# A recurrent mixer's key, reception and value projections computed from high and low parts

## The reference, cut to what matters

```python
def rwkv7_time_mix(h, mix, ...):
    xx = jnp.pad(h, ((0, 0), (1, 0), (0, 0)))[:, :-1] - h
    xr, xw, xk, xv, xa, xg = [h + xx * mix[i] for i in range(6)]
    r = (xr @ w_r).astype(f32)          # 256x1024 @ 1024x1024
    k = (xk @ w_k).astype(f32)
    v = (xv @ w_v).astype(f32)
    w_log = -jax.nn.softplus(-(w0 + jnp.tanh(xw @ w1) @ w2).astype(f32)) - 0.5
    a = jax.nn.sigmoid((a0 + (xa @ a1) @ a2).astype(f32))
    ...
    kk = kk / jnp.maximum(jnp.sqrt(jnp.sum(kk * kk, axis=-1, keepdims=True)), 1e-12)
    k = k * (1.0 + (a - 1.0) * k_a.astype(f32))
    _, y = lax.scan(rwkv7_step, ...)
    ...
    y = y + (jnp.sum(r_h * k_h * r_k, axis=-1, keepdims=True) * v_h).reshape(B, S, D)
```

## Time and profile before

| what | value |
|---|---|
| median of 3 runs | 2742.5 us (2739.02 to 2743.58) |
| profiled execution, span from its first to its last instruction | 2735.7 us |
| what the median has beside that span | 6.8 us |
| PE busy over the span | 98% |
| DVE / ACT / POOL busy | 77% / 47% / 4% |
| the stage, from the first key matmul to the last of `products(0, 1)` | 754.7 to 854.7 us |

### The profile page before, as it was taken

The page is one execution under the profiler, slowest core; times in us unless marked ns, Lnnn a source line. Parts: engine busy times, 40 slices in busy tenths (PEclk is TensorE's granted clock), DMA queues, the critical chain, the costliest instruction groups (busy, mean ns, idle before and its releaser), DMA issues.

```text
span 2735.7 us, 51145 instructions
## 1 busy us (share of the span) xinstructions
PE 2687.7 (98%) x20542; PEld 2491.8 (91%) x20542; DVE 2119.8 (77%) x3212; ACT 1291.1 (47%) x1781; POOL 109.8 (4%) x109
## 2 busy tenths in 40 slices
PE   8999999999999999999999999999999999999999
PEld 7998799999988989999869999986899999859999
DVE  7985589889764647984977878599777787987777
ACT  5335553443442325335565544556554464464443
POOL 0000000000013310000000000000000000000000
PEclk9999999999999999999999999999999999999999
DMA  7764267667431015764424455441345544404454
GB/s 269 277 230 154 85 261 273 228 251 277 160 129 74 1 69 222 276 233 166 157 74 154 169 184 184 155 146 55 109 164 181 180 161 146 154 16 150 158 184 154
DMA packets 61230, 456.21 MB, mean 167 GB/s; under 512 B 6840, under 2 KB 6864, under 8 KB 8736
## 3 DMA queue, kind: packets, MB, share of 16 engines
q1 hardware_dynamic: 54432, 395.83, 40.0%
q0 software_dynamic: 6656, 58.35, 5.3%
HBM read 453.09 MB, written 1.07 MB: 166 GB/s over the span
## 4 chain that ended last, share of the span: by engine, by line
PE 88%; DVE 5%; ACT 3%; DMA 2%; issue 1%; DVEq 0%; SPq 0%; ACTq 0%
PE ps L762 21%; PE ps L601 14%; PE ps L602 14%; PE ps L603 14%; PE ps L1043 3%; PE ps L1440 3%; DMA ring<-in_weights 2%; PE ps L1447 1%; ACT arena L2076 1%; PE ps L1299 1%; PE ps L1133 1%; PE ps L1126 1%; PE ps L544 1%; PE ps L1282 1%; PE ps L537 1%
## 5 line engine op out<-in xcount | busy, mean ns | idle before, releaser
L1612 ACT ACTIVATE w_parts<-ring 128x1024 fp32r<-128x1024 f32 x462 | 462.9, 1052 | 408.3 <-PE ps L601 315.5
L2147 DVE SCALAR_TENSOR_TENSOR w_parts<-ring,w_parts 128x1024 fp32r<-128x1024 f32 x462 | 544.6, 1219 | 53.5 <-ACT w_parts L1612 53.2
L762 PE MATMUL ps<-stream_high,half_parts 128*128 128x256 f32 x2224 | 427.0, 288 | 2.1 <-DVE half_parts L2352 2.1
L2352 DVE SCALAR_TENSOR_TENSOR half_parts<-ring,half_parts 128x1024 fp32r<-128x1024 f32 x225 | 271.8, 1212 | 135.9 <-ACT half_parts L1699 135.0
L762 PEld LDWEIGHTS ps<-stream_high,half_parts 128*128 128x128 f32 x2224 | 351.9, 190 | 7.5 <-issue 6.7
L601 PE MATMUL ps<-act_parts,w_parts 128*128 128x256 f32 x1232 | 347.1, 282 | 1.6 <-DVE w_parts L2147 1.3
L601 PE MATMUL ps<-h_parts,w_parts 128*128 128x256 f32 x1200 | 340.8, 284 | 7.8 <-DVE w_parts L2147 7.8
L603 PE MATMUL ps<-act_parts,w_parts 128*128 128x256 f32 x1232 | 348.0, 282 | 0.0
L602 PE MATMUL ps<-act_parts,w_parts 128*128 128x256 f32 x1232 | 347.5, 282 | 0.0
L602 PE MATMUL ps<-h_parts,w_parts 128*128 128x256 f32 x1200 | 339.5, 283 | 0.0
L603 PE MATMUL ps<-h_parts,w_parts 128*128 128x256 f32 x1200 | 339.5, 283 | 0.0
(11 more groups left out here) (462 smaller groups left out, 5185.3 us busy)
## 6 DMA issues: line engine op xcount, KB each, us to landing
ring<-in_weights SPq DMA_DIRECT2D x374, 1024.0 KB, 4.8
arena<-in_mod_weights POOLq DMA_DIRECT2D x32, 1536.0 KB, 8.2
arena<-in_cond POOLq DMA_DIRECT2D x8, 512.0 KB, 6.4
arena<-toeplitz_rows POOLq DMA_DIRECT2D x1, 1536.0 KB, 12.3
x<-in_x SPq DMA_DIRECT2D x1, 1024.0 KB, 4.9
arena<-in_ctx POOLq DMA_DIRECT2D x1, 1024.0 KB, 5.5
out<-x SPq DMA_DIRECT2D x1, 1024.0 KB, 3.9
const<-in_const SPq DMA_DIRECT2D x1, 975.0 KB, 11.3
```

What stands on the lines that cost most here:

```text
L762: mm = pe.matmul(into, stationary, moving, start=start and n == 0, stop=stop and n == 2, skip_group_check=True)
L1612: a(w_parts[:, to, 0, cols], ring[:, at, cols], ACT.Copy).then_inc(s["w_high"], 1)
L2147: return stt(out=out, in0=whole, scalar=1.0, in1=high, op0=ALU.mult, op1=ALU.subtract)
L2352: stt(out=half_parts[:, u % 3, 1, :], in0=ring[:, (t["tile"] + tile) % RING, half * HALF:(half + 1) * HALF], scalar=1.0, in1=half_parts[:, ...
```

## The change

The three projections become sums of three fp32r products, like the others. Per half tile (128 x 1024, eight blocks; 24 of them):

- ACT copies the half tile into one of three buffers `rw_high` (`weight_highs`), once the tile has landed and, from the fourth on, once PE has begun the half tile before the last (`half_used`).
- DVE subtracts it and writes the rest over the weights in the ring (`weight_lows`, `ring_low` is the ring's own memory seen as fp32r).
- PE runs 24 products in place of eight matmuls, after waiting for `half_low`.

The moving side (the mixed tokens) is split by DVE, four copies and four subtractions per projection (`split_mixed`). The calls are laid into the queues by hand, and `keep(4, 3)` and `mix(4, 3)` move behind the key's evacuation. The small table of ones moves to memory of `h` (`key_spread`).

```diff
+        ring_low = nc.alloc_sbuf_tensor_at("ring_low", [P, RING, TILE], F32R, offset=ring_at)
+        rw_high = [parts("rw_high0", 29760, HALF), parts("rw_high1", 20992, HALF), parts("rw_high2", 22016, HALF)]
+        mixed_parts = {2: (parts("key_high", 2048, KT, S), parts("key_low", 0, KT, S)),
+                       3: (parts("reception_high", 25120, KT, S), parts("reception_low", 18944, KT, S)),
+                       4: (parts("value_high", 0, KT, S), nc.alloc_sbuf_tensor_at("value_low", [P, KT, S], F32R, offset=half_at))}
...
-                def project(i, p):
+                def project_parts(i, p):
+                    high, low = mixed_parts[i]
                     for m in range(2):
+                        u = 8 * (i - 2) + 2 * p + m
+                        pe.wait_ge(s["half_low"], RW_FIRST + u + 1)
                         for k in range(KT):
+                            if p == m == 0 and k % 2 == 0:
+                                pe.wait_ge(s["mix_ready"], LOW_AT[i] + k // 2 + 1)
...
-                            mm = pe.matmul(ps[:, mm_n[0] % 4, m * S:(m + 1) * S], w.take(), mixed[i][:, k, :], start=(k == 0), stop=(k == KT - 1))
+                            w.used(pe.matmul(into, wh, high[:, k, :], start=(k == 0), stop=False, skip_group_check=True))
+                            mm = pe.matmul(into, wh, low[:, k, :], start=False, stop=False, skip_group_check=True)
+                            if k == 0:
+                                mm.then_inc(s["half_used"], 1)
+                            mm = pe.matmul(into, wl, high[:, k, :], start=False, stop=(k == KT - 1), skip_group_check=True)
...
+                def weight_highs(upto):
+                    while split[0] < min(upto, RW_HALVES):
+                        u = split[0]
+                        tile, half = rw_tile + u // 2, u % 2
+                        actv.wait_ge(loaded[tile % RING], 16 * (tile // RING + 1))
+                        if u >= 3:
+                            actv.wait_ge(s["half_used"], RW_FIRST + u - 1)
+                        a(rw_high[u % 3][:], ring[:, tile % RING, half * HALF:(half + 1) * HALF], ACT.Copy).then_inc(s["half_high"], 1)
...
                 keep(1, 4)
+                weight_highs(1)
                 evac(lora[0:64, 0, :], ACT.Tanh, rows=64, m=0)
...
+                    if dst is rw_b:
+                        weight_highs(2)
+                weight_highs(3)
                 keep(3, 0)
+                weight_highs(4)
                 actv.wait_ge(s["rw_pow"], 1)
                 a(grow, cum, ACT.Exp, scale=-DECAY)
+                weight_highs(5)
                 a(shrink, cum, ACT.Exp, scale=DECAY).then_inc(s["rw_decay"], 1)
-                keep(4, 3)
                 for m in range(KT):
                     if m % 2 == 0:
+                        weight_highs(m + 5)
...
+                keep(4, 3)
+                weight_highs(13)
                 keep(5, 5)
+                weight_highs(14)
                 actv.wait_ge(s["table_ss"], 3)
                 a(root16, ps[0:RW_HEADS, 4, 0:S], ACT.Sqrt).then_inc(s["table_sqrt"], 1)
+                weight_highs(20)
...
+                weight_highs(21)
                 value(0)
...
+                weight_highs(23)
                 value(1)
+                weight_highs(24)
                 value(2)
...
+                def weight_lows(upto):
+                    while split[0] < upto:
+                        u = split[0]
+                        v = (slice(None), (rw_tile + u // 2) % RING, slice(u % 2 * HALF, (u % 2 + 1) * HALF))
+                        dve.wait_ge(s["half_high"], RW_FIRST + u + 1)
+                        stt(out=ring_low[v], in0=ring[v], scalar=1.0, in1=rw_high[u % 3][:], op0=ALU.mult, op1=ALU.subtract)\
+                            .then_inc(s["half_low"], 1)
+                def split_mixed(i):
+                    high, low = mixed_parts[i]
+                    for q in range(QUARTERS):
+                        ks = slice(2 * q, 2 * q + 2)
+                        dve.wait_ge(s["mix_ready"], MIXED_AT[i] + q + 1)
+                        link.mark(nc.vector.tensor_copy(high[:, ks, :], mixed[i][:, ks, :]))
+                    link.wait()
+                    for q in range(QUARTERS):
+                        stt(out=low[:, ks, :], in0=mixed[i][:, ks, :], scalar=1.0, in1=high[:, ks, :], op0=ALU.mult, op1=ALU.subtract)\
+                            .then_inc(s["mix_ready"], 1)
+                split_mixed(2)
+                weight_lows(1)
                 for m in range(KT):
+                    if m == 2:
+                        weight_lows(2)
+                    if m == KT - 2:
+                        weight_lows(3)
...
                 tt(cum, cum, mid.unsqueeze(2).broadcast_to((P, 2 * KT, P + 1)), ALU.subtract).then_inc(s["rw_pow"], 1)
+                weight_lows(4)
...
                 ins.then_inc(s["rw_factor"], 1)
+                weight_lows(5)
                 mix(3, 0)
-                mix(4, 3)
+                weight_lows(6)
+                dve.wait_ge(s["rw_decay"], 1)
+                split_mixed(3)
+                weight_lows(8)
                 dve.wait_ge(s["rw_factors"], 1)
                 for p in range(4):
                     dve.wait_ge(s["mm_evac"], mm0 + 11 + p)
                     link.mark(tt(pair(rw_k, p), pair(rw_k, p), pair(k_factor, p), ALU.mult))
+                    weight_lows(9 + p)
+                mix(4, 3)
+                split_mixed(4)
+                weight_lows(13)
                 mix(5, 5)
+                weight_lows(14)
                 receptance(0)
...
                 nc.vector.reciprocal(inverse16, root16).then_inc(s["table_inverse"], 1)
+                weight_lows(15)
                 receptance(1)
+                weight_lows(16)
                 receptance(2)
+                weight_lows(17)
                 for p in range(4):
+                    if p == 2:
+                        weight_lows(18)
...
                 receptance(3)
+                weight_lows(20)
...
                 ins.then_inc(s["rw_rk"], 1)
+                weight_lows(24)
                 dve.wait_ge(s["rw_turn"], 1)
```

More of the change, by code:

```diff
@@ L396, in build @@
         FIRST = dict(halves=[*range(28)], half=0, tile=ffn_tiles[0] + FTILES)
-        halves_first = len(FIRST["halves"])
+        RW_FIRST, RW_HALVES = len(FIRST["halves"]), 24
+        halves_first = RW_FIRST + RW_HALVES
         for t in STREAMS:
@@ L1036, in widen_pair @@
                     done()
-                def project(i, p):
+                def project_parts(i, p):
+                    high, low = mixed_parts[i]
                     for m in range(2):
+                        u = 8 * (i - 2) + 2 * p + m
+                        pe.wait_ge(s["half_low"], RW_FIRST + u + 1)
+                        halves[0] += 1
+                        into = ps[:, mm_n[0] % 4, m * S:(m + 1) * S]
                         for k in range(KT):
-                            if p == 0:
-                                mixed_quarter(i, m, k)
-                            mm = pe.matmul(ps[:, mm_n[0] % 4, m * S:(m + 1) * S], w.take(), mixed[i][:, k, :], start=(k == 0), stop=(k == KT - 1))
-                            w.used(mm)
+                            if p == m == 0 and k % 2 == 0:
+                                pe.wait_ge(s["mix_ready"], LOW_AT[i] + k // 2 + 1)
+                            t, b = divmod(w.n, BLOCKS)
+                            w.take()
+                            wh, wl = rw_high[u % 3][:, k * P:(k + 1) * P], ring_low[:, t % RING, b * P:(b + 1) * P]
+                            w.used(pe.matmul(into, wh, high[:, k, :], start=(k == 0), stop=False, skip_group_check=True))
[3 more added lines that the diff above has]
+                            mm = pe.matmul(into, wl, high[:, k, :], start=False, stop=(k == KT - 1), skip_group_check=True)
                     mm.then_inc(s["mm_ready"], 1)
@@ L1050, in value @@
                     pe.wait_ge(s["rw_r_out"], p + 1)
-                    project(4, p)
+                    project_parts(4, p)
                 narrow(0, (64,), filler=2)
@@ L1058, in rwkv @@
                         widen_pair(lora[:, i:i + 1, :], (64,))
+                assert w.n == rw_tile * BLOCKS
                 for p in range(4):
                     pe.wait_ge(s["mm_evac"], mm_n[0] - 3)
-                    project(2, p)
+                    project_parts(2, p)
                 for p in range(4):
                     pe.wait_ge(s["mm_evac"], mm_n[0] - 3)
-                    project(3, p)
+                    project_parts(3, p)
                     if p == 0:
@@ L1072, in rwkv @@
                         for m in range(KT):
-                            mm = pe.matmul(ps[:, 4 + m // 2, (m % 2) * S:(m % 2 + 1) * S], spread[0][:, m * P:(m + 1) * P], inverse16, start=True, stop=True)
```

(24 more changed lines are left out.)

7 lines of the change are left out of this document (6 added, 1 removed).

## The result

| | before | with the change |
|---|---|---|
| median | 2741.72 us (2739.02 to 2743.58, 4 runs) | 2754.08 us (2753.80 to 2754.44, 4 runs) |
| ratio to before, 95% interval | | 1.0048 [1.0033, 1.0062] |
| span of the profiled execution | 2735.7 us | 2752.4 us |

A forecast was written before the change was run, and what follows sets the result against it. The stage was taken as PE-bound before and DVE-bound after, through DVE's queue ahead of the bonus. 13.6 - 3.9 + 2.4 + 2 = +14.1 us gave a median of 2756.6 us, range 2742 to 2766, likeliest between 2750 and 2765.

The forecast's parts named there:

- The bound turns from PE to DVE: Stage of the three projections: without waits DVE ends `rw_rk` at 826.8, PE stands before the bonus at 813.7; DVE 13 us behind.
- the high part ahead of ACT's tanh: Start of the stage: first high part, 1.05 us on ACT, hidden, as tanh ended at 745.07 and the widening began at 747.59.
- DVE's queue up to `rw_rk`: Ahead of the bonus: 826.8 + 8.3 + 3 = 838.1, where the bonus starts in place of 824.55: +13.6 us.
- own work, splits, low parts 1 to 19: DVE up to `rw_rk`: 40.2 us of own work, 8.2 for two more splits, 19 x 1.2 = 22.8 for low parts.
- held by POOL: DVE ahead of the normed keys: two POOL instructions each take up to 4.15 us from it, 8.3 together; bounds 0 and 15.
- waits and gaps: DVE up to `rw_rk`: 3 us of its own waits, at 799 and at 819 for the seventeenth high part.
- POOL is free: Rival: POOL's two instructions fall into DVE's waits, about 6 us; `rw_rk` at 833, +8 us, 2750; chance 0.22.
- The copies: Behind `rw_rk`: copies releasing `products(0, 0)` queue behind low part 23; 5.0 and 0.2 of hand-overs against 2.8: +2.4 us.
- The clock: Before the bonus: PE idle 8 us halves the clock once, some 4 us at half speed behind: +2 us, bounds 0 and 5.
- The sum: Whole kernel: +14.1 us; span 2735.7 to 2749.8, median, 6.8 above the span before, to 2756.6, 0.5% slower; chance 0.50.
- -3.9 + 2.4: Behind `rw_rk`: 48 remaining value products at 0.434 - 0.353 save 3.9 us; the late copies add 2.4.
- the clock keeps falling: Rival: 10 us of PE's work at half clock where PE is waited for, +10 on top: 2767; chance 0.06.

The follow-up runs named there:

- no_pool: Against the change: GpSimd's two products with shrink left out, and the decay with them; median 2747.43 us, ratio to before 1.0023.
- copies_first: Against the change: DVE's two copies of the transposes go ahead of low parts 22 and 23; median 2748.71 us, ratio to before 1.0030.
- value_reordered: Only value in parts; low parts 18, 19 and gate's mix behind the bonus's products, copies ahead of low parts 22, 23; 2733.02 us, ratio to before 0.9974.
- mix5_late: Against the change: DVE's last mix, for the gate, moved behind the bonus's products; median 2754.24 us, ratio to before 1.0050.
- warm_holes: Against the change: thirteen matmuls of no use on PE right before its wait for the bonus's products; median 2749.39 us, ratio to before 1.0039.
- key_only: Against the change: only the key projection in parts, reception and value plain float32; median 2750.24 us, ratio to before 1.0033.
- reception_only: Against the change: only the reception projection in parts, key and value plain float32; median 2734.79 us, ratio to before 0.9971.
- key_pool_on_dve: Against the change: only the key in parts, and GpSimd's two products done by DVE; median 2737.41 us, ratio to before 0.9996.
- all_reordered: All three in parts, with `value_reordered`'s order, POOL's products on DVE, reception's and value's token high parts on ACT; 2741.93 us, ratio to before 1.0008.
- value_only: Against the change: only the value projection in parts, key and reception plain float32; median 2743.04 us, ratio to before 1.0008.

## Why the prediction came out as it did

*The bound turns from PE to DVE: right, and shown.* The releasers of PE's waits are DVE's, but for the 0.45 us at the start, where the high part ahead of ACT's tanh, which the prediction had as hidden, wasn't quite; and taking DVE's work away or moving it (`no_pool`, `copies_first`, `value_reordered`) shortens the stage.

*DVE's queue up to `rw_rk`.* Forecast end 838.1; measured 841.0 less 2.8, so 838.2. Its terms, from the end of the first low part (low parts and half tiles are counted from 0, as in the code):

| term | forecast | measured |
|---|---|---|
| end of the first low part | 755.6 | 757.9 - 2.8 = 755.1 |
| own work, splits, low parts 1 to 19 | 40.2 + 8.2 + 22.8 = 71.2 | 76.87 - 7.86 = 69.0 |
| held by POOL | 8.3 | 11.11 - 3.25 = 7.9 |
| waits and gaps | 3 | 83.15 - 76.87 = 6.3 |

The end fits to 0.1 us by luck, because two misses cancel. A split takes 1.42 + 2.50 us, and low parts in a row 1.2 less their overlap, so that the work was 2.2 us less; and the waits, 5.6 of them on ACT, were twice the 3 us taken. Four of them, 2.5 us together, stand at the low parts 8 to 11, right behind the stretch in which PE ran at 0.50; one of 2.25 at low part 16. For that one `mix5_late` shows the reason: a high part waits for PE's progress, so when PE is slow ACT holds DVE. The "POOL is free" rival had about 6 us of waits, as it came, but needed the hold to be nothing.

*POOL: the size right, the place wrong.* I had POOL get in where DVE would wait on its own, in `split_mixed(3)`, with the hold spread. It got in between a low part and the mix of the reception, while DVE ran back to back, both instructions in a row, and stretched eight DVE operations by 7.9 us. So in place of four small waits, at half tiles 3 to 6, PE had one of 8.6 us at half tile 5, one of 1.86 at half tile 3 and one of 0.2 later on. The Trainium skill, SBUF — State Buffer, section "Who interferes with whom", says that the order of issue decides who is blocked, for the whole instruction. For this hold the trace agrees: POOL is 0.1 us ahead, DVE's 3.25 us become 11.11, and POOL's 4.26 and 4.33 are not stretched.

*The copies: right.* Forecast 2.4 late, measured 2.09, and `copies_first` takes it away.

*The clock: the term that was too small.* I took 2 us, bounds 0 and 5, from some 4 us at half speed behind one hole; no row of before shows those 4 us. In after the clock was at 0.50 for the first 4 us of work behind the hole before the bonus, and for 5.5 us behind that of 8.6 us. So the size for one fall was about right. But behind the bonus the stage is 2.5 us longer, where -3.9 + 2.4 makes -1.5 without the clock: 4.0 for it. The rows show 2.1 in the bonus's own matmuls (5.73 for 3.60) and 1.7 in `products(0, 0)` (3.68 for 2.00), which is a second fall, behind the wait of only 2.1 us; I had counted one fall. `warm_holes` gives back the first and `copies_first` the second. The second came in four of the six kernels that had this wait, so that the 1.7 us are in part luck. In all, matmuls at the lower clock took some 10 to 12 us more of PE's time in the stage. Most of that lies ahead of the bonus, where PE would have waited for DVE instead, and there it reached the end at most through DVE's 4.8 us of waits for high parts; that wasn't taken apart.

*The sum.* The stage became 16.2 us longer for a forecast of 14.1, the difference being the clock's 2.0. The median moved by 12.4, to 2754.1 for 2756.6. The 2.5 us between don't have a step: they are of the size by which single executions of before differ from its median. The carry-over of 6.8 us from span to median was scatter for the most part: the two differ by 1.7 to 2.0 in each execution, and the rest is that the profiled execution of before was a short one.

*The rival "the clock keeps falling"* came half true: PE runs at 0.50 in 785 to 790 and at 0.66 in 820 to 825, but ahead of a wait for DVE of 6.6 us that takes most of it up. That more than the two falls behind the bonus reached the end isn't shown.

The first 2.8 us, ahead of the changed code, are chance. `mix5_late`, `copies_first` and `warm_holes` are the same code as after up to the stage, and their first widenings begin at 745.72, 746.43 and 749.58, for 750.39 in after and 747.59 before. The granted clock takes part in it: it is 0.98 in 300 to 400 of after and 1.00 in that stretch of before, in the same code.

## What to carry to other kernels

When an edit moves work from the bound engine to one with free time, sum up the second engine's queue up to each point at which the first waits for it, not its share over the stage: DVE had 49 us free here, half of them in the last third of the stage, and 20 of the 24 low parts and three splits had to run ahead of the bonus. Apply such an edit where the room is (the reception alone, or the value alone in its new order, brought 6 us; all three lost 12), and look for other users of a shared port in the stretch that becomes closed. A hole costs its length and often the clock behind it: the wait of 2.1 us cost another 1 to 1.7 us in four kernels of six. And a length taken from one trace has that luck in it; ask whether a second kernel with the same code at that place shows the same.

## What the runs showed of the hardware

- POOL got in between two DVE instructions that followed each other without a gap. Before, one of its products had stood for some 5 us behind back-to-back mixes (9.21 in place of 4.2 us); in after and in `key_only` it began within 0.1 us of DVE's mix and ran at 4.26, and DVE's eight operations took 11.11 both times. So a closed queue of DVE doesn't settle which of the two comes first.
- The granted clock fell with PE busy for 3.00 of 3.00 us, behind sixteen matmuls with 16 rows of weights (0.93, 0.50, 0.50 in `mix5_late`; 0.59 in `reception_only`, whose stage has no wait of PE at all), in a stage that had come through the same group at 1.00 before. It fell behind this group in ten of fourteen kernels, and not in before, `key_pool_on_dve`, `value_reordered` and `all_reordered`. The Trainium skill, TensorE: Matmul & The Clock Gate, section "Part 1: The HAM clock gate", has two levels, half and full; the rows at 0.50 agree, and those between are stretches with both.
- A fall can follow a wait of about 2 us, and needn't. Behind 2.10 us `products(0, 0)` took 3.34 in `warm_holes`, with no wait of over 0.2 us in the 70 us ahead, and 2.00 in `value_only` and `no_pool`, with waits of 3.0 and 5.6 us some 20 us ahead.
